# A hybrid decoder step on one Trainium2 core: first key pages in both rings, a store and a reload in place of a sum, and copies in place of a masked product

## What is computed

```
layer 0 (FoX):   h = rmsnorm(x); q,k,v,f,q_mem,gate = split(h @ w_in)
                 prompt: causal attention with forget decays over 256 positions, 12 heads
                 sample: the same over 2048 cached positions: 16 pages of 128 x (12*128) keys
                         and 16 of values for each of 8 samples, found through page_table
                 both:   attention to 256 memory rows (keys, values = rmsnorm(mem) @ w_mem)
                 x += rmsnorm((concat(o_tok, o_mem) * silu(gate)) @ w_o)
layer 1 (RWKV-7): shifted projections r,k,v; per head (24 heads of 64) the recurrence
                 S = S*w_t + (S @ -kk_t)(kk_t*a_t)^T + v_t k_t^T ;  y_t = S r_t
                 prompt: 256 steps from S = 0;  sample: one step from a given S
                 then group norm, memory attention, gate, w_o and residual as above
```

## Time and profile before

| | us |
|---|---|
| median of 3 runs | 1935.25 (1933.27 to 1936.63) |
| the profiled execution | 1936.76, of which the span 1935.1 |
| PE busy in the span | 1729.2 (89%), granted clock 0.949 |
| DVE / ACT / POOL busy | 995.9 / 358.6 / 200.6 |
| DMA | 421.12 MB, mean 218 GB/s |

### The profile page before, as it was taken

The page is one execution under the profiler, slowest core; times in us unless marked ns, Lnnn a source line. Parts: engine busy times, 40 slices in busy tenths (PEclk is TensorE's granted clock), DMA queues, the critical chain, the costliest instruction groups (busy, mean ns, idle before and its releaser), DMA issues.

```text
span 1935.1 us, 25942 instructions
## 1 busy us (share of the span) xinstructions
PE 1729.2 (89%) x8810; PEld 1302.5 (67%) x8810; DVE 995.9 (51%) x4853; ACT 358.6 (19%) x882; POOL 200.6 (10%) x319
## 2 busy tenths in 40 slices
PE   8999786989889899979979798889999897899996
PEld 6868554666566566658858566666766665678885
DVE  4347457656555655223361666777666776521102
ACT  2021011111111121211012222222222222111011
POOL 0001111222112112110000000000000000010000
PEclk9999988999899999989989899999999998999998
DMA  9249998999999999863450221222222203255431
GB/s 357 88 153 388 420 417 317 418 421 415 409 361 420 412 420 407 304 241 131 163 234 16 92 91 64 80 82 84 83 85 86 84 20 141 90 186 190 159 131 45
DMA packets 89045, 421.12 MB, mean 218 GB/s; under 512 B 28972, under 2 KB 35024, under 8 KB 79184
## 3 DMA queue, kind: packets, MB, share of 16 engines
q0 software_dynamic: 41680, 218.91, 28.4%
q1 hardware_dynamic: 38808, 186.44, 25.2%
q10 hardware_dynamic: 8424, 14.10, 1.9%
HBM read 406.59 MB, written 12.82 MB: 217 GB/s over the span
## 4 chain that ended last, share of the span: by engine, by line
PE 58%; DMA 17%; DVE 14%; ACT 4%; issue 3%; SPq 2%; POOLq 1%; ACTq 0%; POOL 0%; DVEq 0%
PE psum L626 14%; PE psum L678 12%; PE psum L615 10%; DMA kvr<-in_ck 8%; DMA kvr<-in_cv 6%; PE psum L978 6%; PE psum L852 3%; SPq L510 2%; DVE kmT L2059 2%; DVE kmT L2061 2%; PE psum L664 1%; DVE kvr L1713 1%; PE psum L1037 1%; DMA near<-wring 1%; PE psum L1066 1%
## 5 line engine op out<-in xcount | busy, mean ns | idle before, releaser
L1713 DVE CUSTOM_DVE_ANT_0 kvr<-kvr,arena 128x128 f32<-128x128 f32 x1536 | 334.3, 286 | 154.7 <-DMA kvr<-in_ck 154.6
L626 PE MATMUL psum<-hT,wring 128*128 128x264 f32 x1408 | 343.6, 400 | 0.0
L626 PEld LDWEIGHTS psum<-hT,wring 128*128 128x128 f32 x1408 | 268.7, 195 | 79.4 <-issue 30.4
L978 PE MATMUL psum<-hT,kvr 128*128 128x264 f32 x1152 | 297.4, 408 | 0.0
L978 PEld LDWEIGHTS psum<-hT,kvr 128*128 128x128 f32 x1152 | 226.6, 202 | 56.8 <-issue 18.8
L852 PE MATMUL psum<-kvr,arena 128*32 128x384 f32 x1024 | 115.6, 525 | 48.4 <-DMA kvr<-in_cv 44.9
L626 PE MATMUL psum<-gT,wring 128*128 128x256 f32 x512 | 120.8, 393 | 11.2 <-DVE gT L1615 11.2
L678 PE MATMUL psum<-hT,kvr 128*128 128x264 f32 x512 | 123.7, 398 | 4.9 <-DMA kvr<-in_wg 4.9
L1713 DVE DVE_READ_ACCUMULATOR2_ANT arena<- 128x1 f32 x1536 | 124.8, 81 | 0.0
L626 PEld LDWEIGHTS psum<-gT,wring 128*128 128x128 f32 x512 | 98.2, 196 | 35.3 <-DVE gT L1615 11.9
L588 POOL TENSOR_TENSOR gT<-wring 128x512 f32<-128x512 f32 x24 | 39.8, 1675 | 763.6 <-DVE wring L2051 763.6
(11 more groups left out here) (383 smaller groups left out, 2029.8 us busy)
## 6 DMA issues: line engine op xcount, KB each, us to landing
kvr<-in_ck POOLq DMA_DIRECT2D x128, 768.0 KB, 13.5
kvr<-in_cv POOLq DMA_DIRECT2D x128, 768.0 KB, 14.4
kvr<-in_wrkv SPq DMA_DIRECT2D x12, 3072.0 KB, 10.5
wring<-in_wkv SPq DMA_DIRECT2D x12, 2048.0 KB, 11.4
wring<-in_wm SPq DMA_DIRECT2D x8, 2048.0 KB, 11.5
wring<-in_wg SPq DMA_DIRECT2D x8, 2048.0 KB, 12.0
wring<-in_wo SPq DMA_DIRECT2D x8, 2048.0 KB, 8.2
kvr<-in_wg SPq DMA_DIRECT2D x8, 2048.0 KB, 8.6
```

The lines of the kernel that those rows point to most:

```text
L626: last = mm(psum[:, m % 2, 0:n], w[:, k, t * P:(t + 1) * P], rhs[:, k, 0:n], start=(k == 0), stop=(k == KT - 1))
L978: last = mm(psum[:, m % 2, 0:T], w[:, k, t * P:(t + 1) * P], hT[:, k, :], start=(k == 0), stop=(k == KT - 1))
L1713: last = v_.tensor_tensor_reduce(page, page, qb[:, n % 2, h * P:(h + 1) * P], 1.0, 0.0, ALU.mult, ALU.add, S[:, n % 2, j * FH + h:j * FH + ...
```

## The change

Four edits, in the words of the code.

1. The first eight key pages (`FIRST` = `KRING` + `VRING`) go into both rings at once. VectorE scores them four heads at a time (`first_scores`): heads 0 to 3 of all eight after the fifth and sixth query tiles, heads 4 to 7 between later query tiles, heads 8 to 11 in the slots. The spreading of the first sample's queries moves into the wq loop to match. Page 8 and those after it go through `kring` alone, and value pages 0 to 3 are issued with slots 12, 14, 16 and 18 (`V_EARLY`).
2. `steps_of_slots` gives slots weights: 0.4 for the first eight, 0.85 up to slot 18, 1.0 after.
3. `mn` is cut in four steps of four tiles, placed ahead of the memory heads' `O`, and all are ahead of `dm`.
4. In layer 1 the product with the samples' v no longer takes a sum on TensorE: SyncE stores the v columns to memory (`vcols`) and loads them back broadcast into `Z` (semaphore `vb`); `sample_sums` has two calls instead of three. `NM` is zeroed once and its six blocks are copied by ScalarE at the end of a turn, in place of GpSimd's two products with a mask.

```
-            STEPS0 += [("S", 0), ("T", 0), ("S", 1), ("O", 0)] if kind == "k" else [("T", 1), ("S", 2), ("O", 1)]
+            STEPS0 += [("S", 0), ("T", 0), ("S", 1), ("mn", 0), ("O", 0)] if kind == "k" else [("T", 1), ("mn", 1), ("S", 2), ("O", 1)]
-        STEPS0 += [("T", 2), ("S", 3), ("O", 2), ("T", 3), ("dm", MH), ("O", 3)]
-        STEPS0 += [("mn", 0)]
+        STEPS0 += [("T", 2), ("mn", 2), ("S", 3), ("O", 2), ("T", 3), ("mn", 3), ("dm", MH), ("O", 3)]
+FIRST = KRING + VRING
+V_EARLY = {FIRST + KRING + 2 * n: n for n in range(VRING)}
...
+    weight = [0.4 if n < FIRST else 0.85 if n < VSLOT[0] else 1.0 for n in range(LAST_FILL)]
+    ends = [sum(weight[:n + 1]) / sum(weight) for n in range(LAST_FILL)]
-            out[min(int(spent / TOTAL0 * LAST_FILL), SLOTS - 1)].append(part)
+            out[min(sum(e <= spent / TOTAL0 + 1e-9 for e in ends), SLOTS - 1)].append(part)
...
+                sp.wait_ge(sem("mix"), o + 2)
+                for h in range(2):
+                    sp.dma_start(vcols[h].rearrange("s v -> v s"), sx[64 * h:64 * h + 64, 2, NPR:T], allow_slow_non_contiguous=True).then_inc(sem("vb"), 16)
+                sp.wait_ge(sem("vb"), 64 * (o + 1) + 32)
+                if o >= 0:
+                    sp.wait_ge(sem("prepared"), o + 1)
+                for h in range(2):
+                    sp.dma_start(Z[64 * h:64 * h + 64, 1, :], vcols[h].rearrange("(a s) v -> a (s v)", a=1).to_broadcast([64, NS * 64]))\
+                        .then_inc(sem("vb"), 16)
                 blocks(o + 1)
...
-                    if slot >= KRING:
-                        pool.wait_ge(sem("k_used"), slot - KRING + 1)
-                    page("k", kring, "k_full", slot, STREAMS[i], slot - KST[i])
-                if slot in V_AT:
+                    if slot >= FIRST:
+                        pool.wait_ge(sem("k_used"), slot - (FIRST if slot < FIRST + KRING else KRING) + 1)
+                    ring, full = (vring, "v_full") if KRING <= slot < FIRST else (kring, "k_full")
+                    page("k", ring, full, slot, STREAMS[i], slot - KST[i])
+                if slot in V_EARLY:
+                    n = V_EARLY[slot]
+                    page("v", vring, "v_full", n, STREAMS[STREAM_OF[n]], n - KST[STREAM_OF[n]])
+                if slot in V_AT and V_AT[slot] >= VRING:
...
-                    lm = masks[:, K_LM + n * P:K_LM + (n + 1) * P].unsqueeze(1).to_broadcast([P, 4, P])
-                    nc.gpsimd.tensor_tensor(NM[:, n, :, :], GM[:, o % 2, :, 0:P], lm, ALU.mult).then_inc(sem("nm_out"), 1)
...
                 if u == 2:
+                    spread_queries(0, 0)
                     sum_squares(1, oT, NMEM)
...
                 if u == 4:
+                    spread_queries(0, 1)
...
-            for c in range(FH // 4):
-                spread_queries(0, c)
+            spread_queries(0, 2)
...
-                    mm((A, B, A)[n], blockones, Z[:, n % 2, :], start=True, stop=True).then_inc(sem("z_y"), 1)
+                    mm((A, B)[n], blockones, Z[:, 0, :], start=True, stop=True).then_inc(sem("z_y"), 1)
...
+                    for n in range(2):
+                        m = BLK * 2 ** n
+                        if solve:
+                            act.wait_ge(sem("lv_w"), 3 * o + n + 1)
+                        for s in range(0, P, 2 * m):
+                            last = ac(NM[s:s + m, n, :, s + m:s + 2 * m], GM[s:s + m, a, :, s + m:s + 2 * m], ACT.Copy)
+                        last.then_inc(sem("nm_out"), 1)
...
+                    for k in range(4 * at[0], 4 * at[0] + 4):
+                        last = stt(memv[:, k, :], memv[:, k, :], gmem(1)[:, k:k + 1], rsm, ALU.mult, ALU.mult)
+            def first_scores(k, c):
+                if k == 0:
+                    dve.wait_ge(sem("qb_c"), c + 1)
+                if c == 0:
+                    dve.wait_ge(sem(f"k_full{k}" if k < KRING else f"v_full{k - KRING}"), 16)
+                for h in range(4 * c, 4 * c + 4):
+                    page = kvr[:, k * PAGE_W + h * P:k * PAGE_W + (h + 1) * P]
+                    last = v_.tensor_tensor_reduce(page, page, qb[:, 0, h * P:(h + 1) * P], 1.0, 0.0,
+                                                   ALU.mult, ALU.add, S[:, 0, k * FH + h:k * FH + h + 1])
...
-                    for h in range(FH):
+                    for h in range(FH if k >= FIRST else 0):
...
+                    if k < FIRST:
+                        last = first_scores(k, 2)
...
-                    tt(x3(Z[:, 1, :]), i64, bs(v), ALU.mult).then_inc(sem("z_in"), 1)
...
-                    dve.wait_ge(sem("z_y"), 3 * (o + 1) + 2)
-                    ch.do(tt(zt, x3(B), bs(km), ALU.mult))
+                    dve.wait_ge(sem("vb"), 64 * (o + 2))
+                    ch.do(tt(zt, x3(Z[:, 1, :]), bs(km), ALU.mult))
```

More of the change, by code:

```diff
@@ L433, in trunk_step @@
         solvedT = nc.dram_tensor("solved_t", (4, 8, BLK * BLK), F32, kind="Internal").ap()
+        vcols = nc.dram_tensor("vcols", (2, NS, 64), F32, kind="Internal").ap()
         drow = nc.dram_tensor("drow", (FH, 3 * P), F32, kind="Internal").ap()
@@ L575, in _ @@
                         continue
-                    if n >= VRING:
-                        pool.wait_ge(sem("v_used"), n - VRING + 1)
+                    pool.wait_ge(sem("v_used"), n - VRING + 1)
                     page("v", vring, "v_full", n, STREAMS[i], n - KST[i])
[L581 to L586, removed]
-                    lm = masks[:, K_LM + n * P:K_LM + (n + 1) * P].unsqueeze(1).to_broadcast([P, 4, P])
-                    nc.gpsimd.tensor_tensor(NM[:, n, :, :], GM[:, o % 2, :, 0:P], lm, ALU.mult).then_inc(sem("nm_out"), 1)
             pool.wait_ge(sem("y_y"), 2 * RP)
@@ L921, in _ @@
                 if u == 4:
+                    spread_queries(0, 1)
                     pe.wait_ge(sem("lf_fs"), 1)
-                    for c in range(3):
+                    for c in (1, 2, 0):
+                        if c == 0:
+                            pe.wait_ge(sem("qb_c"), 2)
                         out, cols = (Wp, Xp, Vp)[c], slice(c * 512, (c + 1) * 512)
@@ L1399, in _ @@
                 if u == 2:
+                    queries_out(0, 0)
                     root(1, rsm)
@@ L1406, in _ @@
                 if u == 4:
-                    for c in range(3):
-                        act.wait_ge(sem("d_t"), c + 1)
+                    queries_out(0, 1)
+                    for nth, c in enumerate((1, 2, 0)):
+                        act.wait_ge(sem("d_t"), nth + 1)
                         ac(DS.rearrange("p (n h) -> p h n", h=FH)[:, 4 * c:4 * c + 4, :],
                            (Wp, Xp, Vp)[c].rearrange("p (h n) -> p h n", h=4), ACT.Copy).then_inc(sem("lf_d"), 1)
-            for c in range(FH // 4):
-                queries_out(0, c)
+            queries_out(0, 2)
             nth = 0
@@ L1678, in step @@
                 elif name == "mn":
-                    dve.wait_ge(sem("mem_in2"), 16)
-                    scaled_rows(memv, memv, NMEM, gmem(1), rsm)
+                    if at[0] == 0:
+                        dve.wait_ge(sem("mem_in2"), 16)
+                    for k in range(4 * at[0], 4 * at[0] + 4):
+                        last = stt(memv[:, k, :], memv[:, k, :], gmem(1)[:, k:k + 1], rsm, ALU.mult, ALU.mult)
+                    if at[0] == 3:
+                        last.then_inc(sem("n_out"), 1)
                 elif name == "self":
@@ L1695, in step @@
                        ALU.mult).then_inc(sem("gp_out"), 1)
+            def first_scores(k, c):
+                if k == 0:
+                    dve.wait_ge(sem("qb_c"), c + 1)
+                if c == 0:
+                    dve.wait_ge(sem(f"k_full{k}" if k < KRING else f"v_full{k - KRING}"), 16)
[3 more added lines that the diff above has]
+                                                   ALU.mult, ALU.add, S[:, 0, k * FH + h:k * FH + h + 1])
+                return last
             def page_scores(k):
@@ L1699, in page_scores @@
                 x, j = STREAMS[n], k - KST[n]
[L1700 removed]
+                if k >= FIRST:
+                    dve.wait_ge(sem(f"k_full{k % KRING}"), 16 * (k // KRING))
                 if x == MS:
@@ L1898, in _ @@
             queries_normed(5)
+            for k in range(FIRST):
+                first_scores(k, 0)
             inverse_root(1, NMEM, rsm)
+            queries_normed(6)
             scaled_rows(memv, memv, NMEM, gmem(0), rsm)
-            queries_normed(6)
             queries_normed(7)
@@ L1906, in _ @@
             tt(gsq, gpost(0), gpost(0), ALU.mult)
-            for n in range(8, 12):
-                queries_normed(n)
+            queries_normed(8)
+            queries_normed(9)
+            for n in range(2):
+                for k in range(KRING * n, KRING * n + KRING):
+                    first_scores(k, 1)
+                queries_normed(10 + n)
             dve.wait_ge(sem("p_done"), 12)
@@ L2087, in normed @@
```

(7 more changed lines are left out.)

26 lines of the change are left out of this document (13 added, 13 removed).

## The result

| kernel | median (range), us | ratio to before, 95% interval | profiled span |
|---|---|---|---|
| before | 1935.28 (1933.27 to 1936.63, 4 runs) | | 1935.1 |
| changed | 1914.60 (1913.65 to 1915.15, 4 runs) | 0.9892 [0.9876, 0.9907] | 1913.0 |
| changed, timed again | 1916.87 (1915.13 to 1918.22, 4 runs) | 0.9902 [0.9887, 0.9917] | 1916.5 |

The change is 18 to 21 us faster; 1917 was predicted. The median of all eight runs of it is 1915.1 us.

The account below looks back on a forecast made before the run. Page transfers were taken to bound layer 0's slots from 195 us on, with TensorE idle 90 us to 860 us. Terms -7.6 - 9 - 7 + 5 + 0 = -18.6 us from 1936.76 gave 1918.2 profiled, 1917 median; range 1908 to 1927.

Parts of the forecast that it names:

- (a): Layer 0, four more key pages (4 to 7) moved ahead of the stream: 7.6 us gained.
- (b): Layer 0, earlier refills of key pages, using unused transfer time from 130 to 195 us: 9 us gained (3 to 20.4).
- (c): Layer 0 near 300 us, memory norm in steps ahead of the wait for decays: 7 us gained (0 to 11).
- (d): Layer 0, slots from 19 on carry 4.7% more of the prompt's work: 5 us lost (0 to 21).
- (e): Layer 1, v's sum off TensorE and ScalarE's copies: nothing on the path, 0 us (-34 to +24).
- Only moved: Layer 0, TensorE's early steps go to later slots that are then TensorE's: about 2.6 us gained, 1933 us; chance 0.12.
- More comes back: Layer 0 slots, (a) whole, (b) 12.4, (c) 11, nothing lost in (d): 31 us, 1904 us; chance 0.13.
- The stores: Layer 1, stores of v hold SyncE; beyond about 10 us each us costs one in 12 turns: 1965 us; chance 0.07.
- Both clock rivals: Layer 1 turns, TensorE's clock slower, 24 us lost, 1941 us, chance 0.05; or faster, 34 us gained, 1883 us, 0.03.

Follow-up runs that it names:

- light: The changed kernel with still lighter early slots, weights 0.2, 0.7 and 1.0 in place of 0.4, 0.85 and 1.0: 1915.91 us, ratio 0.9900.
- stores3: The changed kernel with each turn's two stores of v's columns done three times in sequence, each pair waited for before the next: 2110.17 us, ratio 1.0908.
- The changed kernel again: The changed kernel timed and profiled once more with nothing edited: 1916.87 us, ratio 0.9902.

## Why the prediction was right

- **(a), 7.6 us: right as far as the rows go.** The four pages have moved by 130 us.
- **(b), 9 us: the step that was too large.** (a) and (b) alone give 8.3 us, and the transfer rates leave some 2 us of it for (b). The prediction took three quarters of the unused transfer time from 130 to 195 us for pages. From 130 to 140 us VectorE, busy for 10.00 of 10.00 us, lets them come at 200 GB/s, where "over 350 GB/s from about 132 us" was said; page 11 was issued at 134.90 us and not by 132. From 140 to 195 us TensorE, busy for 55.00 of 55.00 us, sets the pace of the slots, and the edit alone brings nothing forward there.
- **(c), 7 us: right.** 7.5 alone, 8.8 to 11.0 undone, with the wait gone and back.
- **(d), 5 us lost: wrong sign, or nothing.** Undone it costs 2.4 to 4.7 us. The prediction priced only the fuller late slots and put what the lighter early ones give at nothing: they take TensorE's pace off the stretch from 140 to 195 us, where 22 pages are issued instead of 15. The late slots' period was read where TensorE set the pace, from 318 to 340 us; that the other 125 slots paid for the rest in time in which TensorE waited anyway fits this, but was not tried apart.
- **(e), 0: small gain.** 2 us by the traces, 3 to 5 by the times, from v's sum leaving TensorE, of which the prediction said that TensorE would only wait 1 us longer for the third sum. Mostly it does wait, but one step ahead, in `from_state`; ahead of the third sum the wait shrinks from 39.0 to 37.2 us over the turns. Copies by ScalarE and products off GpSimd are worth nothing, as said.
- **The sum.** 8.3 and 7.5 measured alone, 2.4 to 4.7 for the weights and 2.7 to 5.0 for layer 1 measured by undoing make 21 to 26 us, against 18.2 to 20.7 for all; so the parts overlap a little or their differences carry the spread of some us that equal programs show. That 18.6 was hit to within 2 us is in part luck: (a) and (b) were about 8 too large while (d) and (e) together were 9 to 15 too low.
- **What was to be seen.** Pages 4 to 7 issued by 35.34 us, no wait on the norm, projection at 842.8 (841 said), turns of 51.1 us: as said. The first value page is used at 177.8 us (16 earlier, 20 said), but by the weights and not by the pages: with even slots it is at 191.1, 3 earlier. TensorE idles for 71.9 us (70 said), and for 62.7 in the second profile. The 350 GB/s were not there.
- **The rivals.** "Only moved" (1933 us) is out: 1915 to 1917 us were measured, and even slots are not faster. "More comes back" (1904) is out too, since (b) gives less than its 9 and not more. The stores land 14.1 us behind their issue and not in 10 to 12: slack 5.7 us instead of the 7.7 that the prediction had. Both clock rivals: the granted clock of the turns is 0.93 before and after.

None of the eleven other kernels run here is faster than the changed one by more than the spread; light (1915.91) and it are the same.

## What to carry to other kernels

Unused transfer time ahead of a stream is only worth what the engines in step with it leave of it: price earlier pages by the busy share of the engine that frees the buffers, and of the one that the loop waits for, in the same microseconds, and not by the bandwidth. Here the first was VectorE for 10 us and the second TensorE for 55, and work moved off TensorE in those 55 us let the pages come. A piece of work that stands behind a wait it does not need is the cheapest gain to find: look for the engine's idle time just before a long row, and who waits for that row. Before a slow transfer is put into a queue, measure how much slack the queue has; here beyond 5.7 us each us would have cost 12.

## What the hardware showed

**Stores in 4-byte pieces are slow by themselves.** One pair of stores of v is 1024 pieces in 2 x 2 KB. Behind the pair's 3 MB of weights it lands after 14.2 us (first fence, issued at 1381.7 us in stores3, with the median us to landing last); the second pair, issued at about 1397 when the weights had landed and the DMA engines moved 0 GB/s, still takes 8.0, and the third 10.0:

```profile
vcols<-arena SPq DMA_DIRECT2D x2, 2.0 KB, 14.2
```

```profile
vcols<-arena SPq DMA_DIRECT2D x2, 2.0 KB, 8.0
```

```profile
1394.00:1406.00 12.00, 12.00 (x77) 8.62 (x76) 6.42 (x11) 1.63 (x4) 0.00 (x0) 1.00 0.04 0
```

A block store of 64 pieces of 64 bytes lands in 1.4 us. Whether the size of the pieces or their number makes the difference no run here separates. The Trainium skill, "DMA: Bandwidth & Descriptors", Specifications, says that below 512 bytes the DMA engine reads, modifies and writes; the rows agree with slow small stores, but the 64-byte pieces are under that size too, and how much of the 8 us it is no run here shows.

**Less idle time at a lower clock can be the same time.** Two executions of one program differed by 8 us of TensorE's idle time and by 0.02 of granted clock, and reached layer 0's projection 1.5 us apart (under "The changed kernel again").
